# Prompt tokens transposed early, the last tile in halves, and identity transposes on TensorE at the hand-over to the experts

## The chip, the cores and the metric

The kernel runs on one core of one Trainium2 chip (trn2). The metric is the device time of one execution in microseconds (us), as the median of several runs. One core has five engines that run side by side and meet only at semaphores: TensorE (PE in the rows, its weight loads PEld), VectorE (DVE), ScalarE (ACT), GpSimd (POOL) and SyncE (SP), and 16 DMA engines that they feed.

## What is computed

A one-layer encoder runs over a prompt (1024 tokens) and a sample (512 tokens), each 1024 wide in float32:

```python
h = modulate(x, g_mix, sh_m, sc_m)
x = x + gt_m * token_mixer(h, ...)          # w_in, three mixers, three group norms, w_out
h = modulate(x, g_ffn, sh_f, sc_f)          # rms norm * (1 + scale) + shift
aff = softmax(h @ w_router); gates, idx = top_k(aff.T, cap)   # 16 experts, cap 128 and 64
hid = silu(h[idx] @ w_gate[e]) * (h[idx] @ w_up[e])
ye = (hid @ w_down[e]) * gates;  out.at[idx].add(ye)
y = rms_norm(x + gt_f * out, g_final)
```

Every expert chooses its own 128 prompt tokens and 64 sample tokens, so the sample's routing can end only when its last tile has passed the mixer, and no expert product starts before that.

## The kernel before

Tokens go in tiles of 128 (8 of the prompt, 4 of the sample), the width of 1024 in 8 blocks of 128. Large products are made of split operands: a float32 matrix is copied into a rounded part by ACT ("hi") and the rest is subtracted by DVE ("lo"), and TensorE multiplies hi by hi, hi by lo and lo by hi.

The order is: the prompt's mixer, the prompt's `residual` (tile by tile: `w_out_tile` on TensorE, then `x2 = x + gate * out`, then the modulated `h2`), the sample's mixer, the sample's `residual`, the sample's routing, and then 16 experts in a loop. Each engine's program is written out by hand in this order. The prompt's routing is woven into the steps of the sample's mixer (`z_steps`, numbered n): `ROUNDS` says after which step DVE makes how many of the 16 rounds of top-k (`topk_eight`, three instructions over 48x512 each). Step 10 and 11 are `zu1` and `zu2`, 12 is `zc0`, 13 the gating (`sv`), 17 `za1`, 20 `zc2`. At step 12 DVE first norms `v` (`v_norm`, lines L1668 and L1671), for which the gating products (L1331) wait. PSUM has eight banks; a planner (`bank_plan`) gives each new user the bank whose last fill is oldest.

In `w_out_tile` the three groups of blocks go in the order `NORMS` = (2, 0, 1), each into two banks of 512 columns. ACT drains group 2 into `x2` (L1035), DVE adds groups 0 and 1 (L1840), multiplies all 1024 columns by `gtm_b` (L1848) and adds `xr` (L1851). ACT squares and sums (L1049) and takes the root (L1052), DVE inverts it (L1865) and makes `h2` in two instructions a piece (L1871, L1874). TensorE transposes `h2` (`router_blocks`, L1388), the copies `h2T` are made by ACT (first half, L1013) and DVE (second half, L1815), then come the logits (`router_logits`), their copy by ACT (L1019), `router_tokens` (L1407) and its copy by DVE (L1820).

After the sample's last tile (the twelfth in all) follow its softmax, `affinity_rows` (L1414), eight rounds of top-k over 48x256 (L1921, L1923, L1924), `topk_end`, `index_columns` (L1422, L1423) and `chosen` (L1961 and after). GpSimd fetches the first expert's prompt rows early (L765; they depend on the prompt alone) and its sample rows after `chosen` (L773). ACT has by then copied the first four chunks of expert weights (`split`, L1089; a chunk is 128x2048). DVE subtracts them after `chosen` (`split`, L2044, four times). TensorE transposes the rows of expert 0 (`tokens`, L1494 for the prompt, L1496 for the sample), ACT makes their hi parts (L1094), DVE their lo parts (L2050), and the first product (L1505) starts. A load of expert weights is issued by SP when DVE has split the chunk whose buffer it takes (semaphore `w_split`).

## Time and profile before

| | us |
|---|---|
| median of 3 runs | 1526.52 (1525.94 to 1529.21) |
| the profiled execution | 1527.16 |
| its span in the profile | 1525.4 |

| engine | busy us | share of the span |
|---|---|---|
| PE | 1432.7 | 94% |
| PEld | 1273.6 | 83% |
| DVE | 1033.5 | 68% |
| ACT | 774.9 | 51% |
| POOL | 161.7 | 11% |

Times in the rows are us from the start of the span. A row of the order of time gives start, duration, engine, line and operation, the tiles out<-in, the shape and how many instructions are merged; square brackets give the engine's idle time before it and what ended that. PEclk is the granted TensorE clock as a share of 2.4 GHz, so 0.50 is 1.2 GHz. Matmuls are pipelined: the time from one start to the next tells their pace, their own duration does not.

### The profile page before, as it was taken

What the parts mean: (1) busy time and instruction counts of PE and PEld (TensorE: products, weight loads), DVE (VectorE), ACT (ScalarE), POOL (GpSimd) and SP (SyncE); (2) the same over time, 40 slices, a digit from 0 to 9 for tenths busy, and PEclk for the clock granted to TensorE, in tenths of its full rate; (3) what the DMA queues carried; (4) which work ended last, traced back from release to release, by engine and by line L of the source; (5) the groups of instructions that cost most, each with busy time, mean ns of one, the idle gap of its engine ahead of it and who ended that gap; (6) DMA issues with size and microseconds to landing.
All of it is one profiled execution on the core that took longest, in us unless ns stands there. A gap on an engine that the chain in (4) does not pass through costs nothing.

```text
span 1525.4 us, 22693 instructions
## 1 busy us (share of the span) xinstructions
PE 1432.7 (94%) x8583; PEld 1273.6 (83%) x8583; DVE 1033.5 (68%) x1445; ACT 774.9 (51%) x1016; POOL 161.7 (11%) x128
## 2 busy tenths in 40 slices
PE   2999999999999983999999999999999999999992
PEld 1787777887787862999999999999999999999992
DVE  3421533677769776777777777777777777767776
ACT  4422121523542323666666666656666666666564
POOL 2000000000000001020121021021021122022020
PEclk9999999999999995999999999999999999999996
DMA  9233344555331364687787788788788788778786
GB/s 325 103 119 125 117 147 151 192 170 180 101 106 56 131 226 154 193 265 247 247 271 236 248 267 245 249 270 242 254 258 247 259 251 244 272 244 266 253 276 241
DMA packets 217941, 322.20 MB, mean 211 GB/s; under 512 B 7452, under 2 KB 174440, under 8 KB 217896
## 3 DMA queue, kind: packets, MB, share of 16 engines
q1 hardware_dynamic: 208760, 294.70, 58.4%
q0 software_dynamic: 8064, 26.30, 7.4%
q10 hardware_dynamic: 1072, 0.59, 0.1%
q8 instruction: 30, 0.49, 0.1%
q14 instruction: 15, 0.12, 0.0%
HBM read 290.07 MB, written 31.49 MB: 211 GB/s over the span
## 4 chain that ended last, share of the span: by engine, by line
PE 85%; DVE 7%; ACT 3%; DMA 2%; SPq 1%; issue 1%; POOL 0%; POOLq 0%; DVEq 0%; ACTq 0%
PE ps L1183 26%; PE ps L1505 25%; PE ps L1503 10%; PE ps L1518 4%; PE ps L1526 4%; PE ps L1527 4%; PE ps L1519 4%; PE ps L1522 4%; PE ps L1508 1%; DVE wlo L2044 1%; SPq L610 1%; PE ps L1494 1%; ACT whi L1089 1%; DMA ada_w<-in_w_ada 1%; PE ps L1294 1%
## 5 line engine op out<-in xcount | busy, mean ns | idle before, releaser
L1505 PE MATMUL ps<-xT,whi 128*128 128x384 f32 x2048 | 576.9, 357 | 4.9 <-DVE xT L2050 4.9
L2044 DVE TENSOR_TENSOR wlo<-raw,whi 128x2048 fp32r<-128x2048 f32 x192 | 437.4, 2292 | 191.9 <-ACT whi L1089 191.9
L1503 PE MATMUL ps<-xT,wlo 128*128 128x192 f32 x1792 | 455.4, 254 | 0.0
L1505 PEld LDWEIGHTS ps<-xT,whi 128*128 128x128 f32 x2048 | 368.1, 189 | 5.8 <-issue 5.3
L1089 ACT ACTIVATE whi<-raw 128x2048 fp32r<-128x2048 f32 x192 | 362.3, 1906 | 0.0
L1503 PEld LDWEIGHTS ps<-xT,wlo 128*128 128x128 f32 x1792 | 342.7, 191 | 0.0
L1183 PE MATMUL ps<-hT,wring 128*128 128x512 f32 x1224 | 290.1, 396 | 5.8 <-DVE hT L1636 5.8
L1183 PEld LDWEIGHTS ps<-hT,wring 128*128 128x128 f32 x1224 | 229.7, 190 | 58.8 <-DVE hT L1636 6.2
L1119 ACT ACTIVATE gu_l<-ps 128x384 f32<-128x384 f32 x128 | 62.9, 491 | 160.5 <-PE ps L1505 160.5
L1183 PE MATMUL ps<-wo,Yhl 128*128 128x512 f32 x576 | 135.3, 393 | 1.3 <-ACT h2T L1013 1.0
L1183 PEld LDWEIGHTS ps<-wo,Yhl 128*128 128x128 f32 x576 | 107.0, 188 | 24.0 <-ACT h2T L1013 1.4
L1578 DVE TENSOR_TENSOR wring<-wraw,wring 128x1024 fp32r<-128x1024 f32 x34 | 41.1, 1220 | 102.4 <-ACT wring L827 102.4
L1099 ACT ACTIVATE hid<-hidf 128x192 fp32r<-128x192 f32 x128 | 46.6, 364 | 110.5 <-DVE hidf L2089 109.0
L1518 PE MATMUL ps<-whi,hid 128*128 128x512 f32 x256 | 101.0, 395 | 0.0
L1526 PE MATMUL ps<-whi,hid 128*128 128x512 f32 x256 | 99.8, 390 | 0.0
L1527 PE MATMUL ps<-wlo,hid 128*128 128x512 f32 x256 | 99.7, 390 | 0.0
L1519 PE MATMUL ps<-wlo,hid 128*128 128x512 f32 x256 | 99.7, 390 | 0.0
L752 POOL DMA_INDIRECT acc_d<-ye,iscat x15 | 24.1, 1609 | 618.6 <-DVE ye L2077 618.6
L2084 DVE TENSOR_TENSOR gu<-ps,gu_l 128x384 f32<-128x384 f32 x128 | 70.8, 553 | 22.9 <-ACT gu_l L1119 22.4
L827 ACT ACTIVATE wring<-wraw 128x1024 fp32r<-128x1024 f32 x34 | 35.4, 1054 | 91.1 <-DMA wraw<-in_w_in 76.6
L1522 PE MATMUL ps<-whi,hid 128*128 128x512 f32 x256 | 78.8, 389 | 0.0
L1508 PE MATMUL ps<-xT,wlo 128*128 128x192 f32 x256 | 64.6, 252 | 0.0
(214 smaller groups left out, 1546.1 us busy)
## 6 DMA issues: line engine op xcount, KB each, us to landing
raw<-in_w_gate SPq DMA_DIRECT2D x64, 1024.0 KB, 5.0
raw<-in_w_up SPq DMA_DIRECT2D x64, 1024.0 KB
raw<-in_w_down SPq DMA_DIRECT2D x64, 1024.0 KB, 5.3
wraw<-in_w_in SPq DMA_DIRECT2D x34, 512.0 KB, 6.0
wraw<-in_w_ada SPq DMA_DIRECT2D x32, 512.0 KB, 4.9
ada_w<-in_w_ada SPq DMA_DIRECT2D x16, 512.0 KB, 11.2
acc_d<-x SPq DMA_DIRECT2D x12, 512.0 KB, 2.7
h_d<-h SPq DMA_DIRECT2D x12, 512.0 KB, 4.2
```

What stands on the lines that cost most here:

```text
L1089: act.activation(whi[:, j % SPL, :], raw[:, j % RAW, :], ACT.Copy).then_inc(w_hi, 1)
L1183: return pe.matmul(out, lhsT, rhs, start=start, stop=stop, skip_group_check=True)
L1503: pe.matmul(out[:, 0:CAP], wlo[:, slot, w], xT[:, k, 0:CAP], start=False, stop=False, skip_group_check=True)
L1505: mm = pe.matmul(out[:, 0:2 * CAP], whi[:, slot, w], xT[:, k, :], start=k == 0, stop=k == KB - 1, skip_group_check=True)
L1508: pe.matmul(out[:, 0:CAP], wlo[:, slot, w], xT[:, k, 0:CAP], start=False, stop=False, skip_group_check=True)
L1518: pe.matmul(ps[:, 4 + n, :], hid[:, f, part[0]], whi[:, (8 + k) % SPL, w], start=start, stop=False)
L1519: pe.matmul(ps[:, 4 + n, :], hid[:, f, part[0]], wlo[:, (8 + k) % SPL, w], start=False, stop=False)
L1522: pe.matmul(ps[:, 4 + n, :], hid[:, f, part[1]], whi[:, (8 + k) % SPL, w], start=False, stop=stop)
L1526: pe.matmul(ps[:, 6 + n, :], both, whi[:, (8 + k) % SPL, w], start=start, stop=False)
L1527: mm = pe.matmul(ps[:, 6 + n, :], both, wlo[:, (8 + k) % SPL, w], start=False, stop=stop)
L2044: dve.tensor_tensor(wlo[:, j % SPL, :], raw[:, j % RAW, :], whi[:, j % SPL, :].bitcast(F32), ALU.subtract).then_inc(w_split, 1)
L2084: dve.tensor_tensor(gu[:, f % 2, :, :], ps[:, b:b + 2, 0:CAP], gu_l[:, f % 2, :, :], ALU.add).then_inc(gu_summed, 1)
```

## The change

Seven edits. (1) `ROUNDS`: one round fewer after each of steps 10 and 11, one more after each of 17 and 20. (2) In the sample's last tile TensorE makes the logits of tile 1 and the transposes of tile 2 before the tile's third group, not behind the tile; ACT copies both halves of `h2T` of tiles 1 and 2. (3) DVE drains all three groups of the last tile, gate included, and everything goes in halves of 512 columns with a partial sum of squares for each on ACT; `x2 * gsf` is made before the root is there. (4) GpSimd subtracts the first weight chunk. (5) Prompt rows of expert 0 are transposed and copied by ACT during the top-k; ACT then waits for the sample rows before it copies chunks 2 and 3; DVE splits chunk 1, the prompt rows and the sample rows, and only then chunks 2 and 3. (6) The gathered sample rows need one transpose a pair of blocks, one copy and one subtraction. (7) TensorE transposes the identity 28 times after the fifth of the eight last top-k rounds and 28 times after `index_columns`.

```diff
-ROUNDS = {9: 1, 10: 2, 11: 2, 12: 2, 14: 2, 15: 2, 16: 2, 17: 1, 19: 1, 20: 1}
+ROUNDS = {9: 1, 10: 1, 11: 1, 12: 2, 14: 2, 15: 2, 16: 2, 17: 2, 19: 1, 20: 2}
 # drainer_of
+    if name == "h2T" and key[1] and key[2] in (TL[1] - 3, TL[1] - 2):
+        return "act"
-        return "act" if key[3] == NORMS[0] else "dve"
+        return "act" if key[3] == NORMS[0] and key[1:3] != (1, TL[1] - 1) else "dve"
 # gpsimd, ahead of the sample gather
+            pool.wait_ge(w_hi, 1)
+            pool.tensor_tensor(wlo[:, 0, :], raw[:, 0, :], whi[:, 0, :].bitcast(F32), ALU.subtract).then_inc(w_split, 1)
             pool.wait_ge(first_rows, 1)
 # scalar
+            def last_squares():
+                tt = NT - 1
+                for n, ready in enumerate((x2_first, x2_ready)):
+                    cols = slice(GW * n, GW * (n + 1))
+                    act.wait_ge(ready, 1 if n == 0 else NT)
+                    act.activation(xr[:, tt % 2, cols], x2[:, tt % 2, cols], ACT.Square, accum_out=ssh[:, n:n + 1]
+                                   ).then_inc(half_sum, 1)
+                    if n == 0:
+                        act.wait_ge(half_sum, 1)
+                        act.activation(ss2[:, tt:tt + 1], ssh[:, 0:1], ACT.Identity, bias=eps[:, :], scale=1.0 / D
+                                       ).then_inc(ss2_ready, 1)
+                act.wait_ge(half_sum, 2)
...
                     if s and t == TL[1] - 1:
                         h2T_drain(1, t - 1)
+                        lg_drain(1, t - 1)
+                        last_squares()
+                        continue
...
+            def first_tokens_hi():
+                for k in range(4):
+                    act.wait_ge(prompt_in, k + 1)
+                    act.activation(xT[:, k:k + 5:4, 0:CAP_P], first_of(k, 0, CAP_P), ACT.Copy).then_inc(prompt_hi, 1)
+                act.wait_ge(t_filled, 4)
+                act.activation(xT[:, :, CAP_P:CAP], sample_of(range(KB)), ACT.Copy).then_inc(t_hi, 4)
...
-            for i in range(4):
+            for i in range(2):
                 split(0, i)
-            tokens_hi(0)
+            first_tokens_hi()
+            for i in range(2, 4):
+                split(0, i)
 # tensor
                 for k in NORMS:
+                    if (s, t, k) == (1, TL[1] - 1, NORMS[2]):
+                        router_logits(1, t - 2)
+                        router_blocks(1, t - 1)
...
-                    if t >= 2:
+                    if t >= 2 and (s, t) != (1, TL[1] - 1):
                         router_logits(s, t - 2)
...
-            router_blocks(1, 2)
...
+            def sample_tokens():
+                pe.wait_ge(xe_in, 32)
+                for k in range(4):
+                    pe.transpose(sample_of(range(k, k + 5, 4)), xe[:, 1, P * k:P * (k + 1)], ident[:, :]).then_inc(t_filled, 1)
+                pe.wait_ge(prompt_lo, 4)
+            def keep_clock(n):
+                for _ in range(n):
+                    pe.transpose(bank("warm")[:, 0:P], ident[:, :], ident[:, :])
+            first_tokens()
+            open_bank("xe", GT)
+            open_bank("warm")
+            pe.wait_ge(late_rounds, 1)
+            keep_clock(28)
             index_columns(1)
+            keep_clock(28)
...
             wait_drained(pe, "idx", 1)
-            tokens(0)
+            sample_tokens()
 # vector
+            def last_tile():
...
+                for k in NORMS:
+                    to = x if k == NORMS[0] else h
+                    for n, cols in enumerate(half):
+                        wait_filled(dve, "out", s, t, k, n)
+                        drain(dve.scalar_tensor_tensor(out=to[:, cols], in0=bank("out", s, t, k, n),
+                                                       scalar=rsy[:, tt, k:k + 1], in1=gtm_b[:, cols], op0=ALU.mult,
+                                                       op1=ALU.mult), "out", s, t, k, n)
+                    for n, cols in enumerate(half):
+                        ins = dve.tensor_tensor(x[:, cols], x[:, cols], (xr[:, tt % 2, :] if k == NORMS[0] else h)[:, cols],
+                                                ALU.add)
...
+                for n, cols in enumerate(half):
+                    step(dve.tensor_tensor(h[:, cols], x[:, cols], gsf_b[:, cols], ALU.mult))
+                dve.wait_ge(std_2, NT)
+                step(dve.reciprocal(r, r))
+                for n, cols in enumerate(half):
+                    dve.scalar_tensor_tensor(out=h[:, cols], in0=h[:, cols], scalar=r, in1=shf_b[:, cols], op0=ALU.mult,
+                                             op1=ALU.add).then_inc((h2_first, h2_ready)[n], 1)
+                lt_drain(s, t - 2)
+                lt_drain(s, t - 1)
+                h2T_drain(s, t)
...
+            dve.wait_ge(w_split, 1)
+            split(0, 1)
+            for k in range(4):
+                first_tokens_lo(k)
+            dve.wait_ge(t_hi, 4)
+            dve.tensor_tensor(xT[:, :, CAP + CAP_P:2 * CAP], sample_of(range(KB)), xT[:, :, CAP_P:CAP].bitcast(F32),
+                              ALU.subtract).then_inc(t_lo, 4)
+            for i in range(2, 4):
+                split(0, i)
             dve.wait_ge(gtf_in, 32)
-            for i in range(4):
-                split(0, i)
-            tokens_lo(0)
```

`first_tokens` on TensorE waits for the prompt rows and makes the eight transposes; `first_tokens_lo` on DVE makes their lo parts.

## Rows read from the trace of the kernel before

**Rows 1.** The page's chain that ended last, by engine.
```profile
PE 85%; DVE 7%; ACT 3%; DMA 2%; SPq 1%; issue 1%; POOL 0%; POOLq 0%; DVEq 0%; ACTq 0%
```
**Rows 2.** Who TensorE waited for, 600 to 1526 us: total, times, longest.
```profile
PE ps L1505 <- DVE xT L2050: 4.9, 1, 4.9
```
**Rows 3.** Order of time around the gating of the sample, and of the prompt.
```profile
168.82 5.46 PE L1331 MATMUL ps<-wspT,v 128*64 128x128 f32 x96 [0.17 <-DVE v L1671]
...
454.93 0.20 ACT L921 ACTIVATE ssv<-ssv 128x4 f32<-128x4 f32 x1
455.10 0.69 DVE L1921 MAX8 vals<-aff 48x8 f32<-48x512 f32 x1
...
458.48 1.41 DVE L1671 TENSOR_SCALAR v<-v,ssv 128x384 f32<-128x384 f32 x4
...
459.94 4.51 PE L1331 MATMUL ps<-wspT,v 128*64 128x128 f32 x48 [2.47 <-DVE v L1671]
```
**Rows 4.** Stretches: length, busy of each engine (count), PEclk, DMA share, GB/s.
```profile
460.50:461.00 0.50, 0.50 (x10) 0.50 (x8) 0.49 (x2) 0.00 (x0) 0.00 (x0) 0.50 1.13 343
...
463.50:464.00 0.50, 0.50 (x14) 0.50 (x12) 0.50 (x1) 0.00 (x0) 0.00 (x0) 1.00 0.06 16
```
**Rows 5.** Order of time, DVE and TensorE at the end of the sample's mixer.
```profile
503.75 0.69 DVE L1728 TENSOR_TENSOR zca<-ps,zca 128x512 f32<-128x512 f32 x1 [1.14 <-PE ps L1183]
...
508.99 3.73 PE L1183 MATMUL ps<-wraw,AB 128*128 128x128 f32 x32
509.19 0.69 DVE L1732 TENSOR_TENSOR Y<-ps,cv 128x512 f32<-128x512 f32 x1 [1.92 <-PE ps L1183]
...
509.94 4.07 DVE L1778 SCALAR_TENSOR_TENSOR Yhl<-Y,VT,Yhl 128x512 fp32r<-128x512 f32 x6
```
**Rows 6.** Order of time, the sample's last tile.
```profile
561.50 1.41 DVE L1840 SCALAR_TENSOR_TENSOR x<-ps,rsy,x 128x512 f32<-128x512 f32 x2 [1.31 <-PE ps L1183]
...
562.20 1.09 PE L1388 MATMUL ps<-ident_sb,h 128*128 128x128 f32 x8
...
565.53 1.06 ACT L1049 ACTIVATE h<-x 128x1024 f32<-128x1024 f32 x1 [2.05 <-DVE x L1851]
...
569.42 0.69 DVE L1874 TENSOR_TENSOR h<-h,shf_b 128x512 f32<-128x512 f32 x1
```
**Rows 7.** Order of time, from the copies of the weights to the first product.
```profile
574.74 7.31 ACT L1089 ACTIVATE whi<-raw 128x2048 fp32r<-128x2048 f32 x4
...
583.86 0.40 DVE L1924 MATCH_REPLACE8 aff<-vals,aff 48x256 f32<-48x256 f32 x1
...
590.16 0.23 PE L1422 MATMUL ps<-ident_sb,vals 16*64 16x16 f32 x1 [13.61 <-DVE idxf L1947]
...
591.45 0.98 POOL L773 DMA_INDIRECT xe<-h_d,icur  x1 [27.82 <-DVE icur L1961]
...
591.78 8.90 DVE L2044 TENSOR_TENSOR wlo<-raw,whi 128x2048 fp32r<-128x2048 f32 x4
...
595.01 0.66 PE L1494 MATMUL ps<-ident_sb,xe 128*128 128x128 f32 x2 [4.52 <-DMA xe<-h_d,icur]
...
597.39 0.42 PE L1496 MATMUL ps<-ident_sb,xe 128*128 128x128 f32 x1
...
602.68 0.68 PE L1505 MATMUL ps<-xT,whi 128*128 128x384 f32 x1 [4.87 <-DVE xT L2050]
```
**Rows 8.** Stretches around the first product, columns as in rows 4.
```profile
602.60:606.80 4.20, 4.12 (x16) 4.13 (x17) 0.00 (x0) 0.00 (x0) 0.36 (x2) 0.50 1.09 364
606.80:611.20 4.40, 4.40 (x32) 4.40 (x32) 0.56 (x1) 1.72 (x2) 0.00 (x0) 0.99 0.68 229
```
**Rows 9.** GpSimd in order of time; last, its groups by line (busy, mean ns).
```profile
1.53 0.96 POOL L713 MEMSET brow_r<- 128x1024 f32 x1
...
561.84 0.19 POOL L763 COPY icur<-rowg 128x1 uint32<-128x1 uint32 x1 [285.79 <-PE ps L1183]
...
L747 POOL COPY iscat<-rowid 128x2 uint32 x15 | 16.4, 1096 | 0.0
```

More of the change, by code:

```diff
@@ L228, in bank_events @@
         job("aff", 1, g)
+    for k in range(GT + 1):
+        opened("xe", k)
+    opened("warm")
     job("idx", 1)
@@ L408, in encoder_kernel @@
     smax = small("smax", [TL[0], 1])
+    ssh = small("ssh", [2])
     tick = small("tick", [2])
@@ L556, in encoder_kernel, with first_of, sample_of @@
     w_d = a["w_down"][0].rearrange("e (k p) f -> e p k f", p=P)
+    def first_of(k, first, end):
+        return ps[:, k, 0:2 * CAP].rearrange("p (a n) -> p a n", a=2)[:, :, first:end]
+    def sample_of(blocks):
+        return bank("xe", GT).rearrange("p (k n) -> p k n", k=KB)[:, blocks.start:blocks.stop:blocks.step, :]
     def load_chunk(eng, e, j):
@@ L1010, in h2T_drain @@
             def h2T_drain(s, t):
-                wait_filled(act, "h2T", s, t, 0)
-                wait_h2t_free(act, s, t)
-                drain(act.activation(h2T[:, 0:GT, :].rearrange("p b n -> p (b n)"), bank("h2T", s, t, 0), ACT.Copy),
-                      "h2T", s, t, 0)
+                for half in range(2):
+                    if drainer["h2T", s, t, half] != "act":
+                        continue
+                    wait_filled(act, "h2T", s, t, half)
+                    wait_h2t_free(act, s, t)
+                    drain(act.activation(h2T[:, GT * half:GT * (half + 1), :].rearrange("p b n -> p (b n)"),
+                                         bank("h2T", s, t, half), ACT.Copy), "h2T", s, t, half)
+            def last_squares():
[10 more added lines that the diff above has]
+                act.wait_ge(half_sum, 2)
+                act.wait_ge(ss2_ready, NT)
+                act.activation(rs2[:, tt:tt + 1], ssh[:, 1:2], ACT.Sqrt, bias=ss2[:, tt:tt + 1], scale=1.0 / D
+                               ).then_inc(std_2, 1)
             def lg_drain(s, t):
@@ L1027, in residual @@
                         h2T_drain(s, t - 2)
-                    for h in range(2):
+                    for h in range(2) if tt < NT - 1 else ():
                         wait_filled(act, "out", s, t, NORMS[0], h)
@@ L1866, in residual @@
                     after_step()
-                    parts = 2 if tt == NT - 1 else 1
-                    for n in range(parts):
-                        cols = slice(D // parts * n, D // parts * (n + 1))
-                        hh = h2[:, tt % GT, cols]
-                        step(dve.scalar_tensor_tensor(out=hh, in0=x2[:, tt % 2, cols], scalar=r, in1=gsf_b[:, cols],
-                                                      op0=ALU.mult, op1=ALU.mult))
-                        after_step()
-                        dve.tensor_tensor(hh, hh, shf_b[:, cols], ALU.add).then_inc(h2_first if n + 1 < parts else h2_ready, 1)
+                    hh = h2[:, tt % GT, :]
+                    step(dve.scalar_tensor_tensor(out=hh, in0=x2[:, tt % 2, :], scalar=r, in1=gsf_b[:, :], op0=ALU.mult,
+                                                  op1=ALU.mult))
+                    after_step()
+                    dve.tensor_tensor(hh, hh, shf_b[:, :], ALU.add).then_inc(h2_ready, 1)
                     if s == 0 and t == GT + 1:
@@ L1923, in topk_eight @@
                 step(dve.max_index(idxu[0:HALF_AT + NE, eight], vals[0:HALF_AT + NE, eight], row))
-                step(dve.match_replace(row, vals[0:HALF_AT + NE, eight], row, -2.0))
+                ins = dve.match_replace(row, vals[0:HALF_AT + NE, eight], row, -2.0)
+                if s and n == 4:
+                    ins.then_inc(late_rounds, 1)
+                    dve.wait_ge(late_rounds, 1)
+                else:
+                    step(ins)
             def topk_end(s):
```

61 lines of the change are left out of this document (47 added, 14 removed).

## The prediction

> **What bounds the kernel now.** The first view is the page's chain that ended last: TensorE holds 85% of it, VectorE 7% [rows 1]. So most of the span is products one behind the other, and only the rest can be had by an edit that adds no product. The second view is who TensorE waited for in the expert stage: one wait of 4.9 us, ahead of the first product, and none in the 920 us behind it [rows 2]. The 16 experts are bound by TensorE from their first product on. The change leaves the loop as it is, so whatever brings the first product forward brings the end forward by the same time. The third view is the order of time ahead of that product. The reader is to see three places there: a wait of 2.47 us at the sample's gating [rows 3], the chain VectorE, ScalarE, TensorE behind the last tile [rows 6], and the stretch from the end of the top-k at 590.16 to the first product at 602.68 [rows 7]. The fourth view is the granted clock by stretches: 0.50 at two of these places, while products run [rows 4, 8].
>
> The sum below is made on the profiled execution, 1527.16 us (span 1525.4 and 1.8 around it). It lies 0.64 above the median of the runs shown.
>
> **Edit 1, the rounds.** The gating waits for DVE's scaling of v. DVE comes to it at 458.48, held by its queue: behind steps 10 and 11 stand four top-k rounds. The root that it needs was there at 455.13 [rows 3]. A round is three instructions of about 0.69, so 2.1 us; two of them leave, 4.2 us. Then the root is the later: DVE starts about 455.3, ends 1.4 later at 456.8, and TensorE is through with its products at 459.94 - 2.47 = 457.47. The wait of 2.47 goes. Behind it the 48 gating products take 4.51 at a clock of 0.50 [rows 3, 4]; the prompt's 96 took 5.46 at full clock, so 48 are 2.73 [rows 3]. TensorE had a gap of 2.47 before the clock fell and has none now: 1.78 more. TensorE could be 4.25 earlier.
>
> What is late next is DVE, since the two rounds come back as 4.2 us at steps 17 and 20. DVE's queue is ahead of before by 2.9 to 3.2 us from step 12 on (v is scaled at 456.8 instead of 459.9, and the later of the two engines sets each drain). After step 20 it is behind by about 1.1: za2 is drained at about 503.7 to 504.9 instead of 503.75, and not behind a wait of 1.14 [rows 5]. From there convolution, one addition and the last zb drain follow without the waits of 1.14 and 1.92: the drain starts at about 507.1 and not at 509.19 [rows 5]. The first output products need three of the six lo parts (4.07 for six, so 2.04) behind it: 507.8 + 2.05 = 509.9. They came at 508.99 + 3.5 = 512.5. So 2.5 of the 4.25 arrive. Bounds: 0 (the wait only moves) and 4.25 (DVE keeps up).
>
> **Edits 2 and 3, the last tile.** Logits of tile 1 (0.6) and transposes of tile 2 (about 0.95 from start to start of what follows 562.20) now stand ahead of the last group: the tile's last product ends 1.6 later, at 563.1 in the old time [rows 6]. DVE's work on group 0 (two drains of 0.7, two additions of 0.69) can start when that group is whole, 2.8 ahead of 561.5 and so at 558.8, and behind DVE's 2.8 for group 2; it ends about 562.8 and just keeps up. Behind the last product two drains (1.41) and two full-width instructions take until 565.5, and square, root, inverse and two pairs for h2 until 570.1, 8.6 behind 561.5 [rows 6]. Now: drain 0.7, drain 0.7, addition 0.65 (half of x2 at 565.1), addition 0.65 (565.8), on ACT the first square, a small Identity, the second square and the root, an estimate of 0.75 + 0.2 + 0.75 + 0.3 from the 1.06 of the full square and small ones of 0.2 to 0.3 [rows 3, 6], so some 567.1; inverse 0.2, two instructions of 0.74: h2 whole at 568.8 to 569.0. That is 1.1 to 1.3 earlier. ScalarE has the copy of the logits of tile 2 ahead of the first square; it waits for TensorE until about 564.6, 0.3 of work, and is free in time. DVE has two small copies ahead of its half of the last h2T, free too, because the transposes of that half end later. I take 1.1; bounds -0.3 (DVE does not keep up) and 1.6.
>
> **Edits 4 to 6, the hand-over.** DVE splits four chunks in 8.90 from 591.78, then four token parts, and the product starts at 602.68 [rows 7]. After the change DVE has one chunk (2.23, to 594.0) and four prompt parts of 256 columns (some 0.4 each by the 0.69 of 512 columns [rows 5], 1.6 together) to 595.6. The sample rows are there at 595.0 as before: the gather is issued at 591.45 by what the change leaves alone, 3.5 us earlier [rows 7]. Four transposes 0.5, one copy of 512 columns by ACT 0.6, one subtraction 0.7 [rows 5, 6], three crossings of about 0.1: the first product at 597.1. That is 5.55 earlier, and the path is now the gather, not DVE. Chunks 2 and 3 are copied by ACT behind the sample copy (596.3, 598.2, 600.0, at 1.83 each from the 7.31 for four [rows 7]) and split by DVE at 600.5 and 602.8. TensorE wants them at its third step of eight, 9.1 behind 597.1, at 606.2: covered by 3.4 us. If that cover is gone the cost is what the split is late. The loads of later chunks are issued at the splits: chunk 4 leaves earlier, chunks 6 and 7 about 1.8 later (600.5, 602.8), and are used from 611 on; a load takes some 5 us. GpSimd has the wait for the first copy (576.6) and the subtraction ahead of the sample gather; nothing needs it before 590.4.
>
> What the subtraction costs on GpSimd no row shows. Below: it writes 2048 elements, and a memset of 1024 took 0.96, so 1.9 us. Above: three such streams, 5.8 us [rows 9]. It ends by 582.5, with 8 us to spare; I take nothing for it.
>
> The GPSIMD Engine Reference of the Trainium skill (section 3.1, Elementwise) gives 4497 ns for such an instruction; no row here shows one, and by it the sum would be the same.
>
> **Edit 7, the clock.** In the old profile the products from 602.68 to 606.8 ran at 0.50 [rows 8]: 4.1 us at half pace, a loss of 2.05. The first 28 transposes start when the fifth round ends, 583.86 + 0.43 = 584.3. At the pace of 595.01 to 597.39, eleven steps of 0.216 [rows 7], they last 6.0 at the low clock, to 590.3, against topk_ready at 590.1: at worst 0.2 to 0.4 late. The two rises that rows show came 3.6 and 4.1 us after TensorE began to be busy [rows 4, 8], so it should rise within the batch or just behind it. The second 28 start about 590.8 and end about 594.0. Then come 1.0 idle, 0.5 of transposes and 1.5 idle before the first product. The clock fell in rows after an idle time of 2.5 [rows 3, 4]; here are 2.5 in two pieces. I hold both for possible: 2.05 if it stays up, 0.4 if it falls. I take 1.3; bounds 0 and 2.05, and -2 if the transposes never raise it (the second batch would then run to 596.9 and hold the sample's).
>
> **Sum.** 2.5 + 1.1 + 5.55 + 1.3 = 10.45; 1527.16 - 10.45 = 1516.7, and 1516.1 on the footing of the median. I give 1516.5.
>
> **The rivals.**
> (a) The clock is low at the first product, or the batches stand in the way. For it: 2.5 idle us near the end. Against it: two short pieces instead of one. 1516.7 + 1.3 to 3.3: 1518 to 1520.
> (b) GpSimd's subtraction and DVE hold each other up. For it: GpSimd's copy of 128x2 takes 1096 ns on average beside DVE's long two-input subtractions in the loop, and one of 128x1 took 0.19 with DVE on other work [rows 9]. Against it: in the new order DVE is on the top-k then, which reads one tensor at a time. If each waits out the other, 2 to 5.8 us of the top-k move: about 1520.5. SBUF — State Buffer of the Trainium skill (section SBUF: two separate sides) has this as a rule: one of the two gets a shared pair of ports for a whole instruction and the other blocks, if the DVE instruction has two SBUF inputs or runs in a two-port mode. By that rule the top-k, with one input each, is spared, and the 1096 ns agree with it.
> (c) The rounds give nothing: DVE's queue passes the whole 2.5 back at the end of the mixer. 1519.2. For it: DVE is the late engine at the gating, and waits for TensorE only 1.14 and 1.92 at the other end [rows 3, 5].
> (d) Slower than before: GpSimd's subtraction is much longer than a stream price. It stands ahead of the sample gather on GpSimd and ahead of DVE's split of chunk 1. It begins at 575.5; from 15 us on it delays the gather and the first product one for one, and from 25.5 us the kernel is slower. At 30 us: 1521 + 10 = 1531. Against it: that is 12 ns an element, thirteen times the memset's pace [rows 9].
> (e) The edits move the order of work but the path before the experts ends elsewhere (a bank, a load, ScalarE's wait for the sample rows ahead of chunks 2 and 3), and most of the gain is lost: 1524 to 1528. For it: ScalarE now stands idle from 580 to 595.7 with two copies behind that wait. Against it: the 3.4 us of cover.
>
> **How the numbers follow.** Chances: forecast 0.60, (a) 0.17, (b) 0.07, (c) 0.06, (d) 0.03, (e) 0.07. The range reaches from all bounds good (2.5 + 1.6 + 5.6 + 2.05, and 1 of the DVE bound in edit 1: 12.7 below, 1513.5 on the median's footing) to (b): 1512.5 to 1521. Within 0.2% (3.05 us, about what a measurement can tell from no change) of 1526.52 lies half of (e) and little else: 0.05. Slower by more than that: 0.04, from (d) and the tail of (e). Faster: 0.91.
>
> **What would show it.** In the profile after: no wait ahead of the gating's 48 products, and these in about 2.7 us at clock 1.00; a wait of TensorE for DVE's Yhl of 1 to 2 us ahead of the first output products; h2 of the last tile whole 5.7 behind its last product and not 8.6; the GpSimd subtraction between 575 and 581 at unchanged times of the top-k; the first product 2.1 us behind the landing of the sample rows; the granted clock there. The end of top-k to the first product was 12.5 us and should be 7.0. Wrong would be: a product of expert 0 that waits for a split, or a top-k round longer than 1.37.

## The result and the profile after

| | before | after |
|---|---|---|
| median of 4 runs each, us | 1526.70 (1525.94 to 1529.21) | 1516.90 (1515.15 to 1519.01) |
| ratio after / before | | 0.9936, interval 0.9920 to 0.9952 |
| profiled execution, us | 1527.16 | 1515.15 |
| its span, us | 1525.4 | 1513.3 |
| mean granted clock of TensorE | 0.974 | 0.982 |

The change is faster by 9.8 us, 0.64%. The forecast was 1516.5 in 1512.5 to 1521.

The two profiles lie 12.1 us apart. The table cuts both spans at the same five instructions: the first of the 48 gating products, the first output product (w_out), the first index column behind the top-k, the first transpose of the sample rows, and the first product of the experts. Each row is a difference of two starts that stand in the fences of this section and in [rows 3] and [rows 7]; the one not shown there is the first output product of before:

```profile
512.48 4.34 PE L1183 MATMUL ps<-wo,Yhl 128*128 128x512 f32 x18
```

| stretch | before, us | after, us | after - before |
|---|---|---|---|
| start to the gating | 459.94 | 456.20 | -3.74 |
| gating to first output product | 52.54 | 52.10 | -0.44 |
| to the first index column | 77.68 | 76.12 | -1.56 |
| to the transposes of the sample rows | 4.85 | 4.47 | -0.38 |
| to the first product of the experts | 7.67 | 2.25 | -5.42 |
| to the end | 922.72 | 922.16 | -0.56 |

The page of the profile after, its chain that ended last, by engine:

```profile
PE 83%; DVE 8%; ACT 3%; DMA 2%; SPq 1%; issue 1%; POOL 0%; POOLq 0%; DVEq 0%; ACTq 0%
```

The kernel is bound as before [rows 1]: products one behind the other.

Order of time of the kernel after (start, length, engine, line, operation, what ended the idle time), around the gating of the sample and at its first output product:

```profile
453.97 0.18 DVE L1752 RECIPROCAL ssv<-ssv 128x4 f32<-128x4 f32 x1 [0.29 <-ACT ssv L944]
454.18 1.41 DVE L1755 TENSOR_SCALAR v<-v,ssv 128x384 f32<-128x384 f32 x4
455.50 0.68 DVE L2038 MAX8 vals<-aff 48x8 f32<-48x512 f32 x1
...
456.20 2.84 PE L1385 MATMUL ps<-wspT,v 128*64 128x128 f32 x48
...
508.30 4.34 PE L1237 MATMUL ps<-wo,Yhl 128*128 128x512 f32 x18 [0.99 <-DVE Yhl L1862]
```

The reader is to see three things. VectorE scales v as soon as the root is there, with the top-k round behind it and not ahead. The 48 products carry no wait and take 2.84 us where they took 4.51 behind a wait of 2.47 [rows 3]. And 52 us later there is a new wait of 0.99 for VectorE's Yhl: the two rounds that left the gating have come back there.

The last tile of the sample, VectorE, ScalarE and the first transposes of h2:

```profile
558.70 1.41 DVE L1920 SCALAR_TENSOR_TENSOR h<-ps,rsy,gtm_b 128x512 f32<-128x512 f32 x2 [0.81 <-PE ps L1237]
...
560.02 1.28 DVE L1925 TENSOR_TENSOR x<-x,h 128x512 f32<-128x512 f32 x2
560.73 0.63 ACT L1048 ACTIVATE xr<-x 128x512 f32<-128x512 f32 x1 [0.87 <-DVE x L1925]
561.22 1.28 DVE L1935 TENSOR_TENSOR h<-x,gsf_b 128x512 f32<-128x512 f32 x2
...
561.69 0.61 ACT L1048 ACTIVATE xr<-x 128x512 f32<-128x512 f32 x1
...
562.43 0.29 ACT L1056 ACTIVATE rs<-ssh,ss 128x1 f32<-128x1 f32 x1
562.75 0.16 DVE L1937 RECIPROCAL rs<-rs 128x1 f32<-128x1 f32 x1 [0.25 <-ACT rs L1056]
562.95 1.41 DVE L1940 SCALAR_TENSOR_TENSOR h<-h,rs,shf_b 128x512 f32<-128x512 f32 x2
```

From the drain of the last product at 558.70 to the end of h2 at 564.36 it is 5.66 us. In [rows 6] the same drain starts at 561.50 and h2 is whole at 570.11, 8.6 behind. The halves let the squares of one run beside the additions of the other, and the multiplication by gsf_b stands beside square and root.

From the split on GpSimd to the first product:

```profile
571.00 4.52 POOL L794 TENSOR_TENSOR wlo<-raw,whi 128x2048 fp32r<-128x2048 f32 x1 [10.25 <-ACT whi L1134]
...
574.47 0.42 DVE L2038 MAX8 vals<-aff 48x8 f32<-48x256 f32 x1
...
575.83 0.42 DVE L2038 MAX8 vals<-aff 48x8 f32<-48x256 f32 x1
...
578.66 4.61 PE L1562 MATMUL ps<-ident_sb 128*128 128x128 f32 x28 [6.15 <-DVE aff L2041]
...
584.42 0.20 PE L1479 MATMUL ps<-ident_sb,vals 16*64 16x16 f32 x1 [1.15 <-DVE idxf L2069]
...
584.62 3.27 PE L1562 MATMUL ps<-ident_sb 128*128 128x128 f32 x28
...
585.29 0.99 POOL L796 DMA_INDIRECT xe<-h_d,icur  x1 [9.78 <-DVE icur L2083]
...
585.61 2.29 DVE L2172 TENSOR_TENSOR wlo<-raw,whi 128x2048 fp32r<-128x2048 f32 x1
587.82 1.41 DVE L2153 TENSOR_TENSOR xT<-ps,xT 128x256 fp32r<-128x256 f32 x4
...
588.89 0.63 PE L1556 MATMUL ps<-ident_sb,xe 128*128 128x128 f32 x4 [1.00 <-DMA xe<-h_d,icur]
589.62 0.60 ACT L1141 ACTIVATE xT<-ps 128x512 fp32r<-128x512 f32 x1 [15.81 <-PE ps L1556]
...
590.32 0.69 DVE L2288 TENSOR_TENSOR xT<-ps,xT 128x512 fp32r<-128x512 f32 x1 [1.09 <-ACT xT L1141]
...
591.14 0.44 PE L1589 MATMUL ps<-xT,whi 128*128 128x384 f32 x1 [1.62 <-DVE xT L2288]
...
592.05 4.49 DVE L2172 TENSOR_TENSOR wlo<-raw,whi 128x2048 fp32r<-128x2048 f32 x2 [1.04 <-ACT whi L1134]
```

VectorE is through with its prompt parts at 589.2, ahead of the sample's; the last thing that the first product waits for is now the chain gather, transposes, copy, subtraction. In [rows 7] it was four splits and four token parts on VectorE: 7.67 us behind the transposes of the sample rows, now 2.25. Chunks 2 and 3 are split while TensorE works, and no product of the experts has a wait behind the first.

The granted clock (PEclk) around the first products of after; columns as in [rows 4]:

```profile
591.10:591.60 0.50, 0.46 (x3) 0.46 (x4) 0.00 (x0) 0.50 (x1) 0.50 (x1) 1.00 1.10 385
591.60:592.00 0.40, 0.40 (x4) 0.40 (x4) 0.00 (x0) 0.40 (x2) 0.10 (x2) 0.62 1.05 371
592.00:593.00 1.00, 1.00 (x6) 1.00 (x5) 0.95 (x1) 1.00 (x2) 1.00 (x2) 0.50 0.96 214
...
595.00:596.00 1.00, 1.00 (x8) 1.00 (x8) 1.00 (x1) 0.11 (x1) 0.00 (x0) 0.94 0.43 145
```

The first product starts at full clock (2.4 GHz), but some 0.6 us later the clock falls to 0.50 (1.2 GHz) and stays there until about 595.1. The loss moved and shrank a little against [rows 8], from 4.2 us at 0.50 to 3.4, which is 0.4 us of time; it did not go.

### The profile page after: what moved, and what is told of

Same layout as the page of the kernel before. It is cut to its first block, busy times and chain, and to the rows that moved or that the text cites. A ratio compares the mean times of both kernels' runs of the same rounds, so it can differ in the third digit from the quotient of the medians.

```text
span 1513.3 us, 22821 instructions
## 1 busy us (share of the span) xinstructions
PE 1436.5 (95%) x8639; PEld 1277.9 (84%) x8639; DVE 1032.3 (68%) x1449; ACT 775.0 (51%) x1020; POOL 158.1 (10%) x129
## 4 chain that ended last, share of the span: by engine, by line
PE 83%; DVE 8%; ACT 3%; DMA 2%; SPq 1%; issue 1%; POOL 0%; POOLq 0%; DVEq 0%; ACTq 0%
PE ps L1589 25%; PE ps L1237 24%; PE ps L1587 10%; PE ps L1610 4%; PE ps L1602 4%; PE ps L1611 4%; PE ps L1603 4%; PE ps L1606 4%; PE ps L1592 1%; DVE wlo L2172 1%; PE ps L1578 1%; DVE idxu L2040 1%; SPq L631 1%; DVE vals L2038 1%; DVE aff L2041 1%
```

## Experiments

The theory after the comparison: the rounds are worth about 3 us, the last tile 1.25, the hand-over 5.8, the clock 0.5. The rivals: the gain of the rounds and the tile is given back somewhere; the identity transposes do nothing, or cost the time at which they stand in the way; GpSimd's subtraction is free only because of what VectorE does beside it; the first product is still set by VectorE and not by the gather.

One thing has to be read first. Thirteen of the profiled executions (after and the twelve kernels here) have the same code ahead of the gating but for the rounds that all of them moved, and none has a wait over 0.2 us at it. Yet the gating starts between 456.20 (after, the earliest of all) and 459.75. The later stretches repeat to a few tenths: gating to first output product is 52.10 to 52.12 in all eleven that have after's rounds. So a median of four or five runs carries an uncertainty of one or two us from a part of the program that no experiment touches, and the verdicts below rest on the stretches of the profiles as much as on the medians.

| kernel | median, us | ratio to before (interval) | gating | gating to output | to index column | to transposes of rows | to first product | to the end |
|---|---|---|---|---|---|---|---|---|
| r1_rounds_alone | 1524.44 | 0.9979 (0.9970 to 0.9988) | 458.14 | 52.12 | 77.42 | 4.90 | 7.62 | 923.50 |
| t1_tile_back | 1518.10 | 0.9941 (0.9928 to 0.9955) | 457.67 | 52.12 | 77.35 | 4.47 | 2.25 | 922.24 |
| a1_after_again | 1518.65 | 0.9930 (0.9917 to 0.9944) | 459.54 | 52.11 | 76.34 | 4.43 | 2.25 | 922.83 |
| h2_all_splits_first | 1521.50 | 0.9953 (0.9938 to 0.9968) | 458.40 | 52.10 | 75.96 | 4.45 | 5.49 | 923.40 |
| p1_split_on_dve | 1518.36 | 0.9941 (0.9925 to 0.9956) | 458.37 | 52.10 | 76.08 | 4.46 | 3.21 | 922.28 |
| p2_side_by_side | 1520.12, one run | | 456.81 | 52.10 | 76.36 | 4.45 | 5.76 | 922.82 |
| c1_no_identity | 1518.63 | 0.9941 (0.9928 to 0.9955) | 457.91 | 52.10 | 76.13 | 4.50 | 2.71 | 922.45 |
| c2_second_only | 1516.81 | 0.9931 (0.9915 to 0.9947) | 457.59 | 52.11 | 76.59 | 5.40 | 2.23 | 920.68 |
| c3_first_only | 1517.71 | 0.9935 (0.9920 to 0.9950) | 459.75 | 52.11 | 76.09 | 4.47 | 2.71 | 922.67 |
| c4_filled | 1515.59 | 0.9911 (0.9896 to 0.9926) | 458.48 | 52.10 | 76.34 | 4.43 | 2.25 | 920.80 |
| r3_round_late | 1514.15 | 0.9911 (0.9895 to 0.9926) | 457.31 | 50.87 | 76.55 | 4.45 | 2.25 | 920.77 |
| f1_both | 1515.23 | 0.9918 (0.9904 to 0.9931) | 458.31 | 50.86 | 76.34 | 4.44 | 2.25 | 921.30 |

The six stretches of the profile are cut as in the table above. The kernel before, run beside each group, had medians of 1527.71 (beside r1, t1, c1, p2), 1528.68 (a1, c4, h2, r3) and 1527.57 (f1, p1, c3, c2, on another chip than the first two groups). So ratios, and not medians, are compared between groups.

### The rounds alone

The kernel before with one line changed:

```diff
-ROUNDS = {9: 1, 10: 2, 11: 2, 12: 2, 14: 2, 15: 2, 16: 2, 17: 1, 19: 1, 20: 1}
+ROUNDS = {9: 1, 10: 1, 11: 1, 12: 2, 14: 2, 15: 2, 16: 2, 17: 2, 19: 1, 20: 2}
```

> The kernel before with edit 1 alone. My theory: the profile after shows 3.0 us for it (4.2 at the gating, 1.2 given back where TensorE waits for Yhl), so 1523.5 (1526.5 - 3.0), gating without a wait and at clock 1.00, a wait of TensorE for Yhl of about 1 us. Rival: the gain belongs to the other edits and the queue of VectorE passes it back before the last tile: 1526 to 1527, with a longer wait in the residual of the sample.

Measured: 3.3 us less than before by the medians of 11 and 15 runs (1524.44 against 1527.71), the interval 1.8 to 4.6. Order of time of this kernel at the gating and at the first output products:

```profile
458.14 2.84 PE L1331 MATMUL ps<-wspT,v 128*64 128x128 f32 x48
...
510.26 2.08 PE L1183 MATMUL ps<-wo,Yhl 128*128 128x512 f32 x8 [1.01 <-DVE Yhl L1778]
```

The edit does alone what it does in after: no wait, 48 products in 2.84, 1.01 given back at Yhl. Beside before's own 52.54 from the gating on it has 52.12, and in before the gating waited 2.47: 2.47 + 0.42 = 2.9 us. The rival that the whole gain is handed on to the end of the mixer is out. The expert stage keeps its wait of 4.83 for VectorE, as before.

### The rounds, one of them later still

To see what the 1.0 at Yhl is worth, the last of the prompt's rounds was moved out of the mixer, behind its end, where VectorE waits for a load:

```diff
-ROUNDS = {9: 1, 10: 1, 11: 1, 12: 2, 14: 2, 15: 2, 16: 2, 17: 2, 19: 1, 20: 2}
+ROUNDS = {9: 1, 10: 1, 11: 1, 12: 2, 14: 2, 15: 2, 16: 2, 17: 2, 19: 1, 20: 1}
...
-            assert n_round[0] == CAP_P // 8
+            assert n_round[0] == CAP_P // 8 - 1
             mixers_end(1)
+            topk_eight(0, n_round[0])
```

> The kernel after with the last prompt round not at step 20 but behind the end of the sample's mixer, where VectorE waits 2.5 us for TensorE. My theory: the wait of 1.0 us of TensorE for Yhl goes and nothing takes its place: after less 1.0. Rival: the round holds up the first drains of the sample's tile 0 or its routing's end, and the gain comes back as a wait in the residual: no change.

Order of time of this kernel, the first output products and the moved round:

```profile
508.18 4.34 PE L1237 MATMUL ps<-wo,Yhl 128*128 128x512 f32 x18
...
514.98 0.69 DVE L2038 MAX8 vals<-aff 48x8 f32<-48x512 f32 x1
...
517.70 1.41 DVE L1968 SCALAR_TENSOR_TENSOR x<-ps,rsy,x 128x512 f32<-128x512 f32 x2 [0.60 <-DMA gtm_b<-mod_d]
```

The wait is gone and the stretch is 50.87 and not 52.1: 1.2 shorter, of which some 0.3 may come back by the index columns (76.55, against 76.22 on average and up to 76.59 in the others). The median lies 4.5 below the second run of after, which is more than this edit explains. Between the two profiles 1.4 to 2.1 is the clock (last stretch 920.77 against 922.16 and 922.83), and the gating starts 2.23 earlier by chance. The granted clock of this kernel behind its first product at 591.43:

```profile
592.00:593.00 1.00, 1.00 (x9) 1.00 (x9) 0.66 (x1) 1.00 (x2) 0.78 (x1) 1.00 1.19 298
```

### The last tile undone

After without edits 2 and 3, that is with the order, the drains and the two-instruction h2 of before in the last tile:

```diff
-                if s and t == TL[1] - 1 and k == NORMS[2]:
-                    job("lg", 1, t - 2)
-                    router_blocks(1, t - 1)
...
-    if name == "h2T" and key[1] and key[2] in (TL[1] - 3, TL[1] - 2):
-        return "act"
...
-                    if tt == NT - 1:
-                        last_tile()
-                        continue
```

> The kernel after with edits 2 and 3 taken back (the last tile drained and normed as before). My theory: the last tile is worth 1.25 us (h2 whole 5.7 instead of 8.6 us behind the last product, less 1.6 for what TensorE does ahead of the last group), so 1518.1. Rival: the tile's edits gain nothing, because what follows waits for the second half of h2T either way: 1516.9.

The end of h2 in this kernel:

```profile
558.47 1.41 DVE L1957 SCALAR_TENSOR_TENSOR x<-ps,rsy,x 128x512 f32<-128x512 f32 x2 [1.31 <-PE ps L1231]
...
566.38 0.69 DVE L1991 TENSOR_TENSOR h<-h,shf_b 128x512 f32<-128x512 f32 x1
```

567.07 - 558.47 = 8.6, as before, against 5.66 in after. The medians can't part the two (the intervals overlap). The stretch from the first output product to the index column can: 77.35, 77.42 and 77.68 in the three kernels with the old tile, 75.96 to 76.59 with a mean of 76.22 in the nine others that have after's rounds, after among them. 77.48 - 76.22 = 1.26 us. Of the 2.9 us that the chain behind the last product loses, about 1.7 goes into the logits and transposes that now stand ahead of that product.

### After once more

> The kernel after, unchanged, as the footing for the runs beside it: 1517 to 1518, ratio 0.993 to 0.994. If the clock falls in the same place in every run, near the start of the first products, they run 3 to 4 us at 0.50 in this profile too.

The same kernel measured a second time: ratio 0.9930 beside 0.9936. Behind the gating its profile has the same stretches to 0.2 us, except for the last (922.83 against 922.16), and the same fall of the clock, about 1.0 us behind the first product at 594.67 and again for 3.4 us. Its gating starts 3.34 later than in the first profile of after. That is the spread told of above, and it means that the profile of after shown here is a lucky one by about two us: 1.27 of the 12.1 us between the two profiles (3.74 less the wait of 2.47) comes from stretches that the change doesn't touch.

### All splits ahead of the first product

Chunks 2 and 3 copied and split ahead of the sample tokens, on ScalarE and on VectorE:

```diff
-            for i in range(2):
+            for i in range(4):
                 split(0, i)
             first_tokens_hi()
-            for i in range(2, 4):
-                split(0, i)
...
             dve.wait_ge(w_split, 1)
             split(0, 1)
+            for i in range(2, 4):
+                split(0, i)
             for k in range(4):
                 first_tokens_lo(k)
```

> The kernel after with the order of before at the hand-over: ScalarE copies chunks 2 and 3 ahead of its wait for the sample rows, VectorE splits them ahead of the token parts. My theory: VectorE is then the late engine again, with 2 x 2.23 us more ahead of the sample's subtraction: it is through with the prompt parts at 587.8 + 4.45 + 1.4 = 593.7, so the first product comes at 594.5 instead of 591.1, 3.4 us later: after plus 3.4 to 3.8. Rival: the gather and ScalarE set the time, the order of the splits costs nothing.

Order of time of this kernel:

```profile
587.64 6.70 DVE L2170 TENSOR_TENSOR wlo<-raw,whi 128x2048 fp32r<-128x2048 f32 x3
...
594.26 1.41 DVE L2151 TENSOR_TENSOR xT<-ps,xT 128x256 fp32r<-128x256 f32 x4
...
596.40 0.68 PE L1587 MATMUL ps<-xT,whi 128*128 128x384 f32 x1 [4.87 <-DVE xT L2288]
```

The first product is 5.49 behind the transposes of the rows and not 2.25: 3.24 later, against 3.4 worked out. By the medians it is 2.85 (1521.50 against 1518.65). So the order of the splits carries more than half of the hand-over's 5.8, and in after the gather is the later of the two: VectorE waits 1.09 there for ScalarE's copy of the sample rows (the row at 590.32).

### The first split on VectorE

The subtraction of chunk 0 taken from GpSimd and given back to VectorE, ahead of chunk 1:

```diff
-            pool.wait_ge(w_hi, 1)
-            pool.tensor_tensor(wlo[:, 0, :], raw[:, 0, :], whi[:, 0, :].bitcast(F32), ALU.subtract).then_inc(w_split, 1)
...
-            dve.wait_ge(w_split, 1)
+            split(0, 0)
```

> The kernel after with the first chunk subtracted by VectorE, ahead of chunk 1, and not by GpSimd. My theory: VectorE is through with chunk 1 and the prompt parts at 589.2 in the profile after and the sample's copy is there at 590.3, so 1.1 of the 2.23 us are covered: the first product 1.2 us later, after plus 1.2. Rival: the gather still sets the time: no change.

The first product of this kernel:

```profile
594.22 0.68 PE L1587 MATMUL ps<-xT,whi 128*128 128x384 f32 x1 [2.58 <-DVE xT L2286]
```

3.21 behind the transposes against 2.25: 0.96 us, of the 2.2 that the split takes; the rest lies beside the gather. That is what GpSimd's help is worth here. The two other parts of the hand-over, the early transposes of the prompt rows (edit 5) and the fewer, larger instructions for the sample rows (edit 6), were not run by themselves; what each of them brings is not shown.

### GpSimd and VectorE on two tensors each, side by side

Rival (b) of the prediction did not come true in after. This kernel makes the collision: GpSimd's subtraction of chunk 0 stands behind the sample gather and is held until VectorE begins chunk 1. VectorE's prompt parts wait for both chunks, as in after.

```diff
             pool.wait_ge(w_hi, 1)
+            pool.wait_ge(chunk_one, 1)
             pool.tensor_tensor(wlo[:, 0, :], raw[:, 0, :], whi[:, 0, :].bitcast(F32), ALU.subtract).then_inc(w_split, 1)
...
+            dve.memset(ssr[:, 0:1], 0.0).then_inc(chunk_one, 1)
+            dve.wait_ge(chunk_one, 1)
+            dve.tensor_tensor(wlo[:, 1, :], raw[:, 1, :], whi[:, 1, :].bitcast(F32), ALU.subtract).then_inc(chunk_one, 1)
```

> The kernel after with GpSimd's subtraction of the first chunk put behind the sample gather, so that it runs beside VectorE's subtraction of chunk 1, which no longer waits for it. If one instruction holds the pair of ports whole, either VectorE's 2.29 us becomes 4.5 or more, or GpSimd's 4.52 becomes up to 6.8, and the first product is up to 2.3 us later than GpSimd alone would make it. If they share nothing, both keep 2.29 and 4.52. The kernel as a whole should be 1 to 3 us slower than after, since GpSimd ends at about 590.8.

Order of time of this kernel:

```profile
586.53 2.29 DVE L2287 TENSOR_TENSOR wlo<-raw,whi 128x2048 fp32r<-128x2048 f32 x1
587.20 5.99 POOL L798 TENSOR_TENSOR wlo<-raw,whi 128x2048 fp32r<-128x2048 f32 x1
...
593.32 0.06 DVE L2290 MEMSET ssr<- 128x1 f32 x1 [4.50 <-POOL wlo L798]
```

The same instruction took 4.52 us beside the top-k in after and takes 5.99 here, 1.47 more; VectorE's, which was under way first, keeps its 2.29. VectorE was busy for 1.62 of the time since 587.20, so GpSimd lost about what was left of VectorE's instruction, and the other 4.4 us are close to its 4.52. In after, the top-k rounds beside GpSimd keep their lengths (MAX8 0.42 us, and 1.36 from one round to the next, from 574.47 to 575.83 and also behind GpSimd's end at 575.5). So in this one profile GpSimd was held up by a VectorE instruction with two inputs that was under way, and the top-k, with one, was spared. The other order, VectorE behind a GpSimd instruction under way, is in none of these runs. What is seen agrees with the rule of the Trainium skill, SBUF — State Buffer, section SBUF: two separate sides. The spans of GpSimd are rough in the profile; that VectorE had to wait until 593.32 fixes the end of this one from the other side. The first product came 5.76 behind the transposes and not 2.25, 3.5 later, where 1 to 3 were expected.

### Without the identity transposes, with one batch, and with more

After without both batches:

```diff
-            keep_clock(28)
             index_columns(1)
-            keep_clock(28)
```

> The kernel after without the 56 identity transposes. My theory: they shorten the index columns by 0.4 us (0.38 instead of 0.80) and keep the clock up for part of the first products, here 0.55 us, more where the clock happens not to fall: 1517.9 to 1518.9, first products at 0.50 from their start for 3.4 to 4.2 us or longer. Rival: they buy nothing, since the clock falls anyway at the first products: 1516.9.

Only the second batch, and only the first:

```diff
-            keep_clock(28)
             index_columns(1)
             keep_clock(28)
```

> The kernel after with the second 28 identity transposes only. They begin at the low clock at about 585; at 0.216 us each they would last 6.0 us and with a rise after 3.6 to 4.1 us some 5 us, to 590. The sample rows land at 588.9 (profile after), so their transposes come up to 1 us late, and the clock rises just before the first products and does not fall in the first 3 us: after plus 0 to 1.5. Rival: they hold the sample rows' transposes for the whole 1.1 us and the clock falls all the same: after plus 2 or more.

```diff
             keep_clock(28)
             index_columns(1)
-            keep_clock(28)
```

> The kernel after with the first 28 identity transposes only. My theory: the clock is up at the index columns (0.4 us kept), but falls in the 4 us ahead of the sample rows, so the first products run at 0.50 from their start: 0.4 better than without any, so after plus 0.5 to 1.3. Rival: one batch is enough for all of it: no change against after.

More in the second batch, and a third behind the transposes of the sample rows, so that TensorE is at work in both gaps:

```diff
             index_columns(1)
-            keep_clock(28)
+            keep_clock(38)
...
             sample_tokens()
+            keep_clock(14)
```

> The kernel after with 38 identity transposes instead of 28 behind the index columns, so that they last until the sample rows land, and 14 more between the transposes of the sample rows and the first product. My theory: the clock falls at the first products because of the two idle pieces of 1.0 and 1.6 us ahead of them; with both filled it stays at 1.00 and the 3.4 us at 0.50 go, which is 1.7 us: 1515.2 (after less 1.7), or 0.1 to 0.3 more where the last transposes end behind the sample's subtraction. Rival: the clock falls whatever stands there, because transposes of the identity keep it up only partly: no gain.

Order of time of TensorE in these kernels. Without any batch, the transposes of the sample rows:

```profile
590.64 1.09 PE L1556 MATMUL ps<-ident_sb,xe 128*128 128x128 f32 x4 [4.20 <-DMA xe<-h_d,icur]
```

With the first batch alone, and the granted clock while TensorE waits and at the transposes:

```profile
592.42 1.09 PE L1556 MATMUL ps<-ident_sb,xe 128*128 128x128 f32 x4 [4.21 <-DMA xe<-h_d,icur]
```
```profile
591.00:592.00 1.00, 0.00 (x0) 0.00 (x0) 1.00 (x3) 0.00 (x0) 0.00 (x0) 1.00 0.45 180
592.00:593.00 1.00, 0.58 (x3) 0.61 (x4) 0.76 (x3) 0.00 (x0) 0.00 (x0) 0.64 0.20 63
```

With the second batch alone:

```profile
586.53 5.32 PE L1562 MATMUL ps<-ident_sb 128*128 128x128 f32 x28
591.69 0.60 PE L1556 MATMUL ps<-ident_sb,xe 128*128 128x128 f32 x4
```

With both gaps filled, and the clock behind the first product:

```profile
587.11 4.37 PE L1562 MATMUL ps<-ident_sb 128*128 128x128 f32 x38
591.35 0.63 PE L1556 MATMUL ps<-ident_sb,xe 128*128 128x128 f32 x4
591.81 1.72 PE L1562 MATMUL ps<-ident_sb 128*128 128x128 f32 x14
593.60 0.44 PE L1589 MATMUL ps<-xT,whi 128*128 128x384 f32 x1
```
```profile
594.00:595.00 1.00, 1.00 (x10) 1.00 (x9) 0.50 (x1) 1.00 (x2) 0.70 (x2) 1.00 1.20 356
```

By the stretches of the table: without any batch the clock is 0.50 at the transposes of the rows (1.09 us for four, 0.63 at full clock), so the first product comes 0.46 later than in after, and it and those behind it run slow; the last stretch is 922.45. With the first batch alone the clock had risen, but fell at about 592.3, within the wait of 4.21: the same 0.46 and the same last stretch, 922.67. The first batch by itself is worth nothing. Nor do the index columns gain the 0.4 us that two of the expectations give to the batches: the gather is issued 0.91 behind the first index column without any batch, 0.87 with the first alone and 0.87 in after. With the second alone the batch starts slow (5.32 us, against 3.27 in after) and reaches over the landing of the sample rows: they are transposed 5.40 behind the index column and not 4.45, 0.95 late. But the clock stays up, and the last stretch is 920.68; 0.95 lost, 1.5 to 2.15 won against after's 922.16 and a1's 922.83. With everything filled, nothing is late (4.43 and 2.25) and the last stretch is 920.80.

So the last stretch falls into two groups. With the clock up behind the first product it is 920.68 to 921.30 (c2, c4, r3, f1). Where the clock is low there, it is 922.16 to 923.50 (the other ten, before among them). The time at 0.50 behind the first product explains the difference: it is 3.3 to 3.4 us in after, a1, t1 and p1, and 3.8 to 4.9 in the six others, and half of it is lost, so 1.7 us in after and up to 2.45. With that half taken off, the ten come to 920.4 to 921.1, beside the four with the clock up. The 2.05 worked out from [rows 8] lies within.

By the medians of these four kernels only c4 stands out, at 0.9911. Its interval lies wholly below that of the kernel without any batch (c1, 0.9928 to 0.9955), so filling both gaps against filling none is shown by times too. It overlaps those of after and of the single batches: that a single batch is worth something can't be shown by times, and is said here from the profiles alone.

What is not settled: in after, a1, t1 and p1 both batches ran, TensorE then waited about 1.0, worked 0.6, waited 1.62 (p1: 2.58), and the clock fell, in p1 0.1 us ahead of the first product, in the others 0.6 to 1.0 us behind it. In r3, with 0.98 and 1.62 of idle time, it did not fall. The same two gaps can end either way, so the fall is a matter of more than their lengths. One thing does differ: in r3 the clock rose later in the first batch, which took 5.29 us against 4.61 to 4.78 in the other four, and so 8.3 us ahead of the first product, against 9.3 to 10.4. Whether that spared r3, no run tests; f1, with the same late rise, has its gaps closed. Closing both gaps kept the clock in the two profiles that have them closed, c4 and f1; in c2, where only the first of the two is closed, it stayed up too.

### Both additions together

> The kernel after with the longer and the additional identity transposes and with the last prompt round behind the sample's mixer, both together. My theory: the two act in different places and add up: after less 1.0 for the wait for Yhl and less 1.7 for the clock, so 2.7 below after (ratio to before about 0.991) and no product at 0.50 behind the sample rows. Rival: the late round shifts the places of the clock and the two do not add: the time of the better one alone.

The edits of c4_filled and r3_round_late in one kernel. The profile has both effects, 50.86 and 2.25, and a last stretch of 921.30 with the clock at 1.00 from the first product on, as long as TensorE has products. The ratio, 0.9918, is no better than either alone (0.9911 both): the interval of each is wider than the gain sought, and r3's profile had the clock up already, so beside it f1 has nothing more to show. f1 is faster than after by its profile, by 1.2 for the round and 0.9 to 1.5 for the clock; by its ratio 1.8 to 2.7, from 0.9918 against 0.9936 and 0.9930, where the intervals overlap.

## Why the prediction was right, point by point

**Edit 1, taken at 2.5, got 2.9.** The gating lost its wait and the products their slow clock: 4.51 to 2.84, 1.67 and not 1.78. What VectorE hands back was sized at 1.75 and is 1.23, of which the wait for Yhl is 0.99; r3, which moves one round away, gets the whole 1.23 back. The mechanism and its place were right; the hand-back was too large by half a microsecond. (By the prediction's own figures, 509.9 against 512.5, it was 2.6 that arrive, not 2.5.)

**Edits 2 and 3, taken at 1.1, got 1.25.** h2 is whole 5.66 behind the last product, where 5.7 was written. VectorE kept up: its drain of the last product follows that product directly.

**Edits 4 to 6, taken at 5.55, got 5.8.** From the first index column to the first product it was 12.52 and is 6.72. The chain behind the landing took 2.25, where 2.1 was written. The other 0.4 was in no term: the gather is issued 0.87 behind the first index column and not 1.29. It isn't the identity batches, since the kernel without them has 0.91, and not the rounds, since r1 has 1.29. What else in the change shortens it is open. The 0.5 written for the four transposes is their time at full clock, and that hangs on edit 7: without the batches they take 0.46 more, and edits 4 to 6 are worth 5.3 (4.50 + 2.71 against 12.52). The cover of chunks 2 and 3 held; no product waits for a split.

**GpSimd's subtraction, taken as hidden with 1.9 to 5.8 us, took 4.52.** It ends at 575.5, 9.8 us ahead of the gather that GpSimd issues next. The figure of the Trainium skill that the prediction gave beside its own bounds, 4497 ns (GPSIMD Engine Reference, section 3.1, where it stands for an addition of this size), agrees with this trace. Rivals (b) and (d) fell with it: the top-k kept its pace, and p2 shows a case in which VectorE was on a split. (The 12 ns an element in rival (d) belong to its 25.5 us; its 30 us would be 14.6.)

**Edit 7, taken at 1.3, got 0.56 at most.** This is the term that was mis-sized. The prediction held two outcomes for possible, 2.05 if the clock stays up over the two gaps and 0.4 if it falls, and took a value between. No profile shows such a value: the clock fell or it did not. In both profiles of after it fell, so rival (a) came true in its first part, the clock low at the first products. The time at 0.50 is 3.4 us where it was 4.2, which gives the 0.4 that was written for this case. The last stretch is shorter by 0.56 in the first profile, and longer by 0.11 in a1; what it varies by beside the clock, 0.7 us, is as large as the term. The miss is 0.74 against the sum and not 1.3 or more, and the other terms are each 0.15 to 0.4 larger, so by the first profile the total holds: 2.9 + 1.25 + 5.8 + 0.56 = 10.5 us, where the sum was 10.45; with the last stretch of a1 it is 9.8. That the misses cancel is luck.

**The rest of the 12.1 us between the profiles** is 1.27 ahead of the gating, plus 0.3 between the first output product and the last tile. The medians, which carry less of that, say 9.8. That the forecast of 1516.5 lies only 0.4 from 1516.90 is in part luck, since a median of four runs moves by more than that.

## What to carry to other kernels

Cut the span at a few instructions that both kernels have and compare the stretches: here they repeat within tenths of a microsecond while the whole moves by three and a half, so they settle edits of one microsecond that no median does. Ahead of a product that waits for several chains, order each engine's queue by when TensorE wants the result and leave what is wanted late behind it (3.24 of the 5.8 us here); then see which chain is last, since more help to any other is worth nothing. Work given to TensorE only to hold its clock has to reach close to the first real product: a batch that left it idle for 4.2 us bought nothing, with idle pieces of 1.0 and 1.6 us left the clock fell in three profiles of four, with only the last 1.6 or none left it stayed up in all three, and the batch that overran the data cost 0.95.

## What the runs showed of the hardware that was not expected

- A GpSimd subtraction of 128x2048 takes 4.52 us beside a top-k on VectorE, and 5.99, in the one profile of that kind, when it meets a VectorE subtraction with two inputs that is under way; VectorE's 2.29 doesn't change.
- The same two idle pieces of TensorE, about 1.0 and 1.6 us with 0.6 of transposes between, were followed by a fall of its clock in three profiles and by none in a fourth.
- Transposes of the identity alone raised the clock of TensorE: in after it went from 0.50 to 1.00 2.8 us into the first batch, in c2 4.2 us into the second. The prediction had kept a case in which they never raise it.
- The first 456 us of the program vary by 3.55 us from one execution to another with the same instructions, while the 52 us that follow vary by 0.02 in the eleven with the same rounds. The start of the first transposes of x varies by 1.8 among them (22.74 to 24.56) and that of the prompt's gating products by 2.3 (167.64 to 169.90), so part of the spread arises behind each; what makes it was not followed.
